# Two transformer blocks on one core: the start addresses of TensorE's large operands become multiples of 256 bytes

## The chip, the cores and the metric

The kernel runs on one core of one Trainium2 chip. The time is device microseconds of one execution of the whole program; it is given as the median of three runs. Below, TensorE is PE in the profile (PEld for its weight loads), VectorE is DVE, ScalarE is ACT, GpSimd is POOL and SyncE is SP.

## The reference, cut to what matters

512 tokens of width 1024 go through two blocks in fp32. The first block has a mixer (S5 and SSD), cross attention over 256 memory tokens, and a feed-forward layer of width 2816; the second has an HGRN2 and a forgetting-attention mixer and a mixture of 16 experts of width 512. What carries most of the work are plain products of activations and weights:

```
proj = rmsnorm(x, mix_norm_w) @ w_in          # 1024 x 2828
x = x + concat(y_s5, y_ssd) @ w_out           # 1024 x 1024
q = h @ wq; k = mem_n @ wk; v = mem_n @ wv    # 1024 x 1024 each
x = x + (silu(causal_dwconv(gv[:, :FF])) * gv[:, FF:]) @ w_down,  gv = h @ w_up
u = rms_norm(x) @ w_in_2
for e in range(16):
    h = silu(t @ w_gate[e]) * (t @ w_up[e])
    y = y + gates[:, e:e+1] * (h @ w_down[e])
```

## The kernel before

An fp32 product is made of three fp32r products. Each operand is split into a high part, its fp32r rounding, and a low part, the fp32 value less the high part: w_hi and w_lo for weights, h_hi and h_lo (or h2_hi and h2_lo, a_hi and a_lo, m_hi and m_lo, xh and xl, hh and hl) for activations. The product is high by high, low by high and high by low, accumulated in one bank of PSUM. In `pe_fm` (L430) these are L447, L448 and L449: 128 x 128 weights are stationary, and 512 columns of activations (256 for the memory) are the moving operand. In `pe_tm` (L454) at L466 to L468 it is the other way round, with 256 columns of weights moving. In the experts (`pe_part`, L3015) 128 x 128 of the gathered rows are stationary and 512 columns of weights move, at L3025 to L3027.

Weights come in slots of 2048 fp32 per partition (1 MB over 128 partitions). SyncE loads slot g into one of three buffers w_raw; ScalarE makes the high part of it into one of two buffers w_hi (`act_split`, L363), VectorE the low part into w_lo (`dve_split`, L371), and TensorE uses them. The waits form a ring: a load waits for the low part of three slots earlier, a high part for the load and for the last product of two slots earlier, a low part for the high part, a product for the low part. In the experts the six parts of an expert have a raw buffer each (three raw_b, three w_raw) and a split pair each: hi_b and lo_b for parts 0 and 1, w_hi and w_lo for parts 2 and 3, and the space of h_hi and h_lo for parts 4 and 5. GpSimd gathers the expert's rows (512 KB) for 12 of the 16 while the experts run, and stores 512 KB of results for each.

The order of instructions is written out engine by engine; no scheduler changes it. Addresses in SBUF are set by hand too: `Memory` (L171) places each tensor at the next multiple of 64 bytes, from offset 16512 up, and stages lay other tensors over the same space. The start of an operand within its tensor is a multiple of 512 bytes for all large products (and of 32 for the eight columns at L1838 to L1840), so the remainder of the tensor's offset modulo 256 is the remainder of the operand:

```
tensor                        offset before   modulo 256   used as
w_raw, w_hi, w_lo             16512 ...          128       weights
h_hi, h_lo, a_hi, m_hi, m_lo  90240 ...          128       activations (w_in, w_out, wo, w_out2; down; memory)
xh, xl                        73856 ...          128       gathered rows of the experts, stationary
h2_hi, h2_lo                  131392, 147776      64       activations (wq, up, all of w_in_2)
a_lo                          205120              64       down projection
raw_b, hi_b, lo_b             145856 ...         192       parts 0 and 1 of an expert
hh, hl                        221632, 223680     192       hidden values of an expert, stationary
```

Of the 1128 blocks of three products with 512 moving columns in `pe_fm`, 376 use h, 576 use h2 and 176 use a_hi and a_lo; the feed-forward has 352 of h2 and 176 of a. 64 blocks of the memory have 256 columns. `pe_tm` has 64 blocks with m as the stationary operand and 128 with h2.

## Time and profile before

| | before |
|---|---|
| median of 3 runs | 1576.21 us (1576.1 to 1580.75) |
| profiled execution | 1577.06 us, span 1575.9 us |
| instructions | 17703 |
| TensorE busy, matmul | 1464.7 us (93%) |
| TensorE busy, weight loads | 1162.5 us (74%) |
| VectorE, ScalarE, GpSimd busy | 1025.3, 759.0, 121.2 us |
| HBM read, written | 213.66 MB, 16.78 MB |

Busy time of a matmul runs from its start to its modelled end, and the next one starts before that end. How long a matmul holds TensorE is therefore read from the difference of two start times in the timeline, here called the pitch. The program's names are shown without the digits that number buffers, so that h_hi in a row can be h_hi or h2_hi; the stage tells which.

### The profile page before, as it was taken

Reading aid. Unit: us, or ns where it says so; the run is one execution under the profiler, and the core shown is the slowest. Engines: PE = TensorE matmul, PEld = TensorE weight load, DVE = VectorE, ACT = ScalarE, POOL = GpSimd, SP = SyncE. Lnnn points to the kernel's source line nnn. Section 1 sums busy time; section 2 is a strip of 40 time slices with the busy share of each in tenths; the row PEclk is TensorE's granted clock in tenths of the full one; section 3 lists DMA queues with packets and bytes.
Section 4 is the critical chain, followed back from the end, with each engine's and each line's share of the span. In section 5 each row is a group of like instructions: output and inputs, shape, how many; then the busy total and the mean of one; then the engine's idle time right before and its main releaser. Section 6 shows DMA issues by size and latency. Waiting matters only on the chain.

```text
span 1575.9 us, 17703 instructions
## 1 busy us (share of the span) xinstructions
PE 1464.7 (93%) x6975; PEld 1162.5 (74%) x6975; DVE 1025.3 (65%) x1361; ACT 759.0 (48%) x999; POOL 121.2 (8%) x148
## 2 busy tenths in 40 slices
PE   7899989889989999999999999899999799999981
PEld 5776668668767788888888778787758688888871
DVE  4888885555335555446555647865655898888976
ACT  5453354644334422222324543235564788887863
POOL 0500000000000000000000202300000101111012
PEclk9989999999999999999999999999999899999996
DMA  6212222202112332232223231111005799999975
GB/s 210 79 63 80 80 99 104 93 1 107 58 50 85 130 147 80 87 130 93 86 74 109 82 107 54 54 54 54 27 1 200 260 414 413 412 408 414 398 295 186
DMA packets 39330, 231.58 MB, mean 147 GB/s; under 512 B 4400, under 2 KB 5696, under 8 KB 17104
## 3 DMA queue, kind: packets, MB, share of 16 engines
q1 hardware_dynamic: 30640, 200.09, 33.9%
q0 software_dynamic: 7648, 27.87, 4.7%
q10 hardware_dynamic: 960, 2.49, 0.5%
q8 instruction: 56, 0.92, 0.2%
q14 instruction: 26, 0.21, 0.0%
HBM read 213.66 MB, written 16.78 MB: 146 GB/s over the span
## 4 chain that ended last, share of the span: by engine, by line
PE 74%; DVE 13%; ACT 6%; issue 4%; DMA 2%; POOL 0%; POOLq 0%; ACTq 0%; DVEq 0%
PE bank L447 14%; PE bank L448 14%; PE bank L449 14%; PE bank L3025 5%; PE bank L3027 5%; PE bank L3026 5%; PE bank L593 2%; DVE w_lo L374 2%; PE bank L466 1%; PE bank L467 1%; PE bank L468 1%; ACT w_hi L368 1%; PE bank L2275 1%; PE bank L2254 1%; PE bank L833 1%
## 5 line engine op out<-in xcount | busy, mean ns | idle before, releaser
L447 PE MATMUL bank<-h_hi,w_hi 128*128 128x512 f32 x952 | 387.1, 407 | 12.8 <-DVE w_lo L374 9.9
L448 PE MATMUL bank<-h_lo,w_hi 128*128 128x512 f32 x952 | 376.9, 396 | 0.0
L449 PE MATMUL bank<-h_hi,w_lo 128*128 128x512 f32 x952 | 376.8, 396 | 0.0
L374 DVE TENSOR_TENSOR w_lo<-w_raw,w_hi 128x2048 fp32r<-128x2048 f32 (+3 forms) x86 | 188.2, 2188 | 90.6 <-ACT w_hi L368 90.0
L447 PEld LDWEIGHTS bank<-h_hi,w_hi 128*128 128x128 f32 x952 | 180.6, 190 | 64.7 <-DVE w_lo L374 13.2
L449 PEld LDWEIGHTS bank<-h_hi,w_lo 128*128 128x128 f32 x952 | 180.4, 190 | 42.1
L448 PEld LDWEIGHTS bank<-h_lo,w_hi 128*128 128x128 f32 x952 | 180.9, 190 | 40.7 <-issue 2.2
L368 ACT ACTIVATE w_hi<-w_raw 128x2048 fp32r<-128x2048 f32 (+3 forms) x87 | 154.6, 1777 | 62.7 <-PE bank L449 62.7
L3210 DVE TENSOR_TENSOR h_lo<-w_raw,h_hi 128x2048 fp32r<-128x2048 f32 x32 | 73.1, 2291 | 13.8 <-ACT h_hi L3111 13.8
L3210 DVE TENSOR_TENSOR lo_b<-raw_b,hi_b 128x2048 fp32r<-128x2048 f32 x32 | 73.1, 2287 | 7.6 <-ACT hi_b L3111 7.6
L448 PE MATMUL bank<-a_lo,w_hi 128*128 128x512 f32 x176 | 69.0, 392 | 0.0
L1656 ACT ACTIVATE gc<-gc 128x512 f32<-128x512 f32 x22 | 13.9, 632 | 113.8 <-DVE gc L970 113.8
L447 PE MATMUL bank<-a_hi,w_hi 128*128 128x512 f32 x176 | 68.7, 390 | 0.0
L449 PE MATMUL bank<-a_hi,w_lo 128*128 128x512 f32 x176 | 68.5, 389 | 0.0
L3111 ACT ACTIVATE hi_b<-raw_b 128x2048 fp32r<-128x2048 f32 x32 | 61.2, 1912 | 5.3 <-PE bank L3027 3.5
L3111 ACT ACTIVATE h_hi<-w_raw 128x2048 fp32r<-128x2048 f32 x32 | 61.0, 1910 | 0.0
L3025 PE MATMUL bank<-h_hi,hh 128*128 128x512 f32 x128 | 52.6, 411 | 4.1 <-DVE hl L3240 2.6
L3025 PE MATMUL bank<-hi_b,xh 128*128 128x512 f32 x128 | 51.8, 405 | 1.4 <-DVE xl L3217 1.4
L3026 PE MATMUL bank<-h_hi,hl 128*128 128x512 f32 x128 | 51.3, 401 | 0.0
L3027 PE MATMUL bank<-h_lo,hh 128*128 128x512 f32 x128 | 51.2, 400 | 0.0
L1690 DVE TENSOR_TENSOR gc<-gc,bank 128x512 f32<-128x512 f32 x22 | 15.1, 688 | 55.1 <-PE bank L449 53.0
L3027 PE MATMUL bank<-lo_b,xh 128*128 128x512 f32 x128 | 50.2, 392 | 0.0
(592 smaller groups left out, 2843.9 us busy)
## 6 DMA issues: line engine op xcount, KB each, us to landing
w_raw<-in_params_dram SPq DMA_DIRECT2D x122, 1024.0 KB, 5.0
raw_b<-in_params_dram SPq DMA_DIRECT2D x51, 1024.0 KB, 7.7
w_raw<-in_params_dram SPq DMA_DIRECT2D x16, 704.0 KB, 4.1
result_rows<-osb POOLq DMA_DIRECT2D x16, 512.0 KB, 8.2
result_rows<-prm POOLq DMA_DIRECT2D x8, 512.0 KB, 3.2
xt<-in_x_t_dram POOLq DMA_DIRECT2D x1, 2048.0 KB, 9.3
scratch_rows<-htm SPq DMA_DIRECT2D x4, 512.0 KB, 3.0
out_dram<-pr SPq DMA_DIRECT2D x4, 512.0 KB, 2.6
```

The costliest lines, as they stand in the source:

```text
L368: A.activation(k.w_hi[:, g % SPLIT, 0:size], k.raw[:, g % RAW, 0:size], ACT.Copy).then_inc(s.w_hi, 1)
L374: V.tensor_tensor(k.w_lo[:, g % SPLIT, 0:size], k.raw[:, g % RAW, 0:size], k.w_hi[:, g % SPLIT, 0:size].bitcast(F32), ALU.subtract).then_i ...
L447: PE.matmul(ps, wh, hi[:, c, 0:width], start=c == 0, stop=False)
L448: PE.matmul(ps, wh, lo[:, c, 0:width], start=False, stop=False)
L449: m = PE.matmul(ps, wl, hi[:, c, 0:width], start=False, stop=c == parts - 1)
L466: PE.matmul(ps, xh, wh, start=c == 0, stop=False)
L593: return k.nc.tensor.transpose(out, in_, k.ident[0:n, 0:n])
L3025: PE.matmul(o, xh[:, k0 + c, :], wh, start=first and c == 0, stop=False)
L3026: PE.matmul(o, xl[:, k0 + c, :], wh, start=False, stop=False)
L3027: m = PE.matmul(o, xh[:, k0 + c, :], wl, start=False, stop=final and c == 3)
L3111: done(A.activation(w_hi[n], raws[n], ACT.Copy), "w", n, c)
L3210: done(V.tensor_tensor(w_lo[n], raws[n], w_hi[n].bitcast(F32), ALU.subtract), "w", n, c)
```

## The change

Class `Memory` gets a method `line` that moves the next offset up to a multiple of 256. It is called ahead of w_raw, ahead of xbc (whose space h2_hi and h2_lo share), and ahead of hi_b. The small tensors row, eps and rt go to the gap in front of w_raw. w_hi and w_lo, each one tensor with two buffers, become two tensors each at the same distance. gates, slot_of, table, act_scrap, ss and pri go behind the hidden values of the experts, and L, eoff and qi into the space of the masks tri and stri, whose last reader is TensorE at L1854. The engines' programs are the same, instruction by instruction and wait by wait; operands change their address, and w_hi and w_lo their names.

```
tensor                        offset after    modulo 256
w_raw, w_hi, w_lo             16896 ...            0
h_hi, h_lo, a_hi, m_hi, m_lo  90624 ...            0
xh, xl                        74240 ...            0
h2_hi, h2_lo                  131584, 147968       0
a_lo                          205312               0
raw_b                         145600             192
hi_b, lo_b                    170240 ...           0
hh, hl                        221440, 223488       0
```

```diff
--- before.py
+++ after.py
@@ -32,6 +32,7 @@
 OVER = MAXCH - E
 SLOT_TILES = MAXCH + 1
 SMALL = -1.0e30
+LINE = 256
 
 
 
@@ -186,6 +187,9 @@
         assert self.at <= self.end, (name, self.at, self.end)
         return t
 
+    def line(self):
+        self.at = (self.at + LINE - 1) // LINE * LINE
+
 
 class Core:
     def __init__(self, nc, ins, out, dram):
@@ -198,21 +202,25 @@
         self.bank = [nc.alloc_psum_tensor(f"bank{i}", [P, 512], F32) for i in range(8)]
         self.act_slot = self.dve_slot = 0
         m = Memory(nc, 16512)
+        self.row, self.eps, self.rt = m("row", [P, NROWS]), m("eps", [P, 1]), m("rt", [P, 4, TT])
+        m.line()
         self.raw = m("w_raw", [P, RAW, SLOT])
-        self.w_hi, self.w_lo = m("w_hi", [P, SPLIT, SLOT], F32R), m("w_lo", [P, SPLIT, SLOT], F32R)
+        self.w_hi, self.w_lo = [[m(f"{n}{i}", [P, SLOT], F32R) for i in range(SPLIT)] for n in ("w_hi", "w_lo")]
         x_at = m.at
         self.xt = m("xt", [P, DB, T])
         h_at = m.at
         self.hi, self.lo = m("h_hi", [P, DB, T], F32R), m("h_lo", [P, DB, T], F32R)
-        self.prm, self.row = m("prm", [P, NCOLS]), m("row", [P, NROWS])
+        self.prm = m("prm", [P, NCOLS])
         self.wr = m("w_router", [P, DB, 20])
-        self.ident, self.ones, self.tri, self.stri = (m(n, [P, P]) for n in ("ident", "ones", "tri", "stri"))
-        self.eps = m("eps", [P, 1])
+        self.ident, self.ones = (m(n, [P, P]) for n in ("ident", "ones"))
+        tri_at = m.at
+        self.tri, self.stri = (m(n, [P, P]) for n in ("tri", "stri"))
         base = m.at
 
 
 
         self.rs, self.dtr = m("rs", [P, T]), m("dtr", [P, TT, SSD_H])
+        m.line()
         xbc_at = m.at
         self.xbc, self.sz = m("xbc", [P, XBC_B, T]), m("sz", [P, 6, T])
         kv_at = m.at
@@ -304,19 +312,21 @@
         m = Memory(nc, x_at, h_at)
         self.xh, self.xl = m("xh", [P, 2, DB, P], F32R), m("xl", [P, 2, DB, P], F32R)
         m = Memory(nc, base)
-        self.xtm, self.gates, self.slot_of = m("xtm", [P, TT, D]), m("gates", [P, 2, TT]), m("slot_of", [P, 2, TT], I32)
-        self.table, self.act_scrap, self.rt = m("table", [P, OVER + 2], I32), m("act_scrap", [P, 2]), m("rt", [P, 4, TT])
+        self.xtm = m("xtm", [P, TT, D])
         inner = m.at
         self.raw_b = m("raw_b", [P, 3, SLOT])
+        m.line()
         self.hi_b, self.lo_b = m("hi_b", [P, 2, SLOT], F32R), m("lo_b", [P, 2, SLOT], F32R)
         rows = m.at
         self.xg, self.osb = m("xg", [P, 2, D]), m("osb", [P, 2, D])
         hidden = m.at
         self.hid = m("hid", [P, EH])
         self.hh, self.hl = m("hh", [P, EH // P, P], F32R), m("hl", [P, EH // P, P], F32R)
-        self.ss, self.pri, self.eoff = m("ss", [P, TT, DB]), m("pri", [P, 4]), m("eoff", [P, 2, E])
-        self.qi, self.qf = m("qi", [P, E], I32), m("qf", [P, E])
-        self.L, self.r4 = m("L", [P, TT, 20]), m("r4", [P, 6, TT, 4])
+        self.gates, self.slot_of, self.table = m("gates", [P, 2, TT]), m("slot_of", [P, 2, TT], I32), m("table", [P, OVER + 2], I32)
+        self.act_scrap, self.ss, self.pri = m("act_scrap", [P, 2]), m("ss", [P, TT, DB]), m("pri", [P, 4])
+        after_tri = Memory(nc, tri_at, tri_at + 4 * P)
+        self.L, self.eoff, self.qi = after_tri("L", [P, TT, 20]), after_tri("eoff", [P, 2, E]), after_tri("qi", [P, E], I32)
+        self.qf, self.r4 = m("qf", [P, E]), m("r4", [P, 6, TT, 4])
         self.r16 = m("r16", [P, 6, TT, E])
         self.tokid, self.tok_f, self.tok = m("tokid", [P, TT], I32), m("tok_f", [P, TT]), m("tok", [P, SLOT_TILES], I32)
         self.tok_next, self.rk, self.over = m("tok_next", [P, 1], I32), m("rk", [P, 4, 2, TT]), m("over", [P, OVER + 1])
@@ -348,7 +358,7 @@
         return self.row[:, slice(*ROWS[name])].rearrange("p (o h) -> p o h", o=1).broadcast_to([P, t, h])
 
     def w(self, g, at, n):
-        return self.w_hi[:, g % SPLIT, at:at + n], self.w_lo[:, g % SPLIT, at:at + n]
+        return self.w_hi[g % SPLIT][:, at:at + n], self.w_lo[g % SPLIT][:, at:at + n]
 
 
 
@@ -365,13 +375,13 @@
     A.wait_ge(k.w_load[g % RAW], 16 * (g // RAW + 1))
     if g >= SPLIT:
         A.wait_ge(s.gemm, FINAL_BLOCK[g - SPLIT] + 1)
-    A.activation(k.w_hi[:, g % SPLIT, 0:size], k.raw[:, g % RAW, 0:size], ACT.Copy).then_inc(s.w_hi, 1)
+    A.activation(k.w_hi[g % SPLIT][:, 0:size], k.raw[:, g % RAW, 0:size], ACT.Copy).then_inc(s.w_hi, 1)
 
 
 def dve_split(k, g):
     V, s, size = k.nc.vector, k.s, SIZES[g]
     V.wait_ge(s.w_hi, g + 1)
-    V.tensor_tensor(k.w_lo[:, g % SPLIT, 0:size], k.raw[:, g % RAW, 0:size], k.w_hi[:, g % SPLIT, 0:size].bitcast(F32), ALU.subtract).then_inc(s.w_lo, 1)
+    V.tensor_tensor(k.w_lo[g % SPLIT][:, 0:size], k.raw[:, g % RAW, 0:size], k.w_hi[g % SPLIT][:, 0:size].bitcast(F32), ALU.subtract).then_inc(s.w_lo, 1)
 
 
 def act_split_half(k, g, half):
@@ -381,7 +391,7 @@
     if half == 0:
         A.wait_ge(k.w_load[g % RAW], 16 * (g // RAW + 1))
         A.wait_ge(s.gemm, FINAL_BLOCK[g - SPLIT] + 1)
-    m = A.activation(k.w_hi[:, g % SPLIT, half * n:half * n + n], k.raw[:, g % RAW, half * n:half * n + n], ACT.Copy)
+    m = A.activation(k.w_hi[g % SPLIT][:, half * n:half * n + n], k.raw[:, g % RAW, half * n:half * n + n], ACT.Copy)
     if half:
         m.then_inc(s.w_hi, 1)
         k.act_slot += 1
@@ -395,7 +405,7 @@
     if half == 0:
         V.wait_ge(s.w_hi, g + 1)
     at = slice(half * n, half * n + n)
-    m = V.tensor_tensor(k.w_lo[:, g % SPLIT, at], k.raw[:, g % RAW, at], k.w_hi[:, g % SPLIT, at].bitcast(F32), ALU.subtract)
+    m = V.tensor_tensor(k.w_lo[g % SPLIT][:, at], k.raw[:, g % RAW, at], k.w_hi[g % SPLIT][:, at].bitcast(F32), ALU.subtract)
     if half:
         m.then_inc(s.w_lo, 1)
         k.dve_slot += 1
@@ -2908,7 +2918,7 @@
 
 def moe_parts(k):
     raws = [k.raw_b[:, i, :] for i in range(3)] + [k.raw[:, i, :] for i in range(3)]
-    w_hi, w_lo = ([x[:, i, :] for i in range(2)] + [w[:, i, :] for i in range(2)] + [flat2(h[:, 4 * i:4 * i + 4, :]) for i in range(2)]
+    w_hi, w_lo = ([x[:, i, :] for i in range(2)] + [w[i][:, :] for i in range(2)] + [flat2(h[:, 4 * i:4 * i + 4, :]) for i in range(2)]
                   for w, h, x in ((k.w_hi, k.hi, k.hi_b), (k.w_lo, k.lo, k.lo_b)))
     return raws, w_hi, w_lo
```

## Rows read from the trace of the kernel before

**Rows 1.** the page's first part: busy us (share of the span) xinstructions of TensorE
```profile
PE 1464.7 (93%) x6975; PEld 1162.5 (74%) x6975; DVE 1025.3 (65%) x1361; ACT 759.0 (48%) x999; POOL 121.2 (8%) x148
```

**Rows 2.** the chain that ended last, shares of the span by line
```profile
by line: PE bank L447 14.3%; PE bank L448 14.0%; PE bank L449 13.9%; PE bank L3025 5.0%; PE bank L3027 4.9%; PE bank L3026 4.9%; issue 4.1%; PE bank L593 2.5%; DVE w_lo L374 2.3%; PE bank L466 1.4%; PE bank L467 1.2%; PE bank L468 1.2%; ACT
```

**Rows 3.** two windows (us): busy time of each engine, granted clock, DMA share, GB/s
```profile
600.00:900.00 300.00, 300.00 (x1293) 242.60 (x1292) 161.80 (x180) 91.32 (x95) 5.42 (x11) 1.00 0.27 90
...
1300.00:1440.00 140.00, 140.00 (x657) 115.36 (x656) 124.56 (x79) 112.65 (x95) 18.34 (x16) 1.00 1.01 411
```

**Rows 4.** the page's groups: operands, shapes, count | busy, mean ns | idle before
```profile
L3210 DVE TENSOR_TENSOR h_lo<-w_raw,h_hi 128x2048 fp32r<-128x2048 f32 x32 | 73.1, 2291 | 13.8 <-ACT h_hi L3111 13.8
L3210 DVE TENSOR_TENSOR lo_b<-raw_b,hi_b 128x2048 fp32r<-128x2048 f32 x32 | 73.1, 2287 | 7.6 <-ACT hi_b L3111 7.6
...
L449 PE MATMUL bank<-a_hi,w_lo 128*128 128x512 f32 x176 | 68.5, 389 | 0.0
...
L3025 PE MATMUL bank<-h_hi,hh 128*128 128x512 f32 x128 | 52.6, 411 | 4.1 <-DVE hl L3240 2.6
```

**Rows 5.** timeline of TensorE (start, duration, us), output projection of the first mixer
```profile
352.19 0.39 PE L448 MATMUL bank<-h_lo,w_hi 128*128 128x512 f32 x1
...
368.51 0.39 PE L448 MATMUL bank<-h_lo,w_hi 128*128 128x512 f32 x1
```

**Rows 6.** timeline of TensorE, up projection
```profile
606.88 0.39 PE L448 MATMUL bank<-h_lo,w_hi 128*128 128x512 f32 x1
...
623.21 0.39 PE L449 MATMUL bank<-h_hi,w_lo 128*128 128x512 f32 x1
```

**Rows 7.** timeline of TensorE, down projection
```profile
664.17 0.39 PE L447 MATMUL bank<-a_hi,w_hi 128*128 128x512 f32 x1
...
677.90 0.39 PE L447 MATMUL bank<-a_hi,w_hi 128*128 128x512 f32 x1
```

**Rows 8.** timeline of TensorE, one expert's parts
```profile
1300.37 0.40 PE L3026 MATMUL bank<-h_hi,hl 128*128 128x512 f32 x1
...
1305.74 0.39 PE L3025 MATMUL bank<-w_hi,xh 128*128 128x512 f32 x1
...
1311.19 0.40 PE L3025 MATMUL bank<-hi_b,xh 128*128 128x512 f32 x1
...
1313.96 0.38 PE L593 MATMUL bank<-ident,hid 128*128 128x128 f32 x2
```

**Rows 9.** timeline of TensorE, products of 256 columns
```profile
253.10 0.28 PE L466 MATMUL bank<-w_hi,m_hi 128*128 128x256 f32 x1
...
254.54 0.28 PE L466 MATMUL bank<-w_hi,m_hi 128*128 128x256 f32 x1
...
938.27 0.28 PE L468 MATMUL bank<-w_lo,h_hi 128*128 128x256 f32 x1
...
940.99 0.28 PE L468 MATMUL bank<-w_lo,h_hi 128*128 128x256 f32 x1
```

**Rows 10.** timeline of TensorE, products with 8 stationary columns
```profile
926.00 0.40 PE L1838 MATMUL bank<-h_hi,w_hi 128*8 128x512 f32 x1
...
931.33 0.39 PE L1840 MATMUL bank<-h_hi,w_lo 128*8 128x512 f32 x1
```

**Rows 11.** timeline of TensorE, plain fp32 products, two merged in a row
```profile
396.19 0.59 PE L1431 MATMUL bank<-kt,qt 128*128 128x256 f32 x2
396.62 0.59 PE L1432 MATMUL bank<-kt,qt 128*128 128x256 f32 x2
```

**Rows 12.** transfers: 40 slices of 1204 to 1216 us, and issues of 1300 to 1440
```profile
GB/s 0 0 0 0 191 246 27 164 382 382 437 410 382 437 437 437 437 410 355 410 437 382 410 410 437 437 437 410 437 437 437 437 437 410 437 437 437 437 437 219
...
raw_b<-in_params_dram SPq DMA_DIRECT2D x24, 1024.0 KB, 8.4
w_raw<-in_params_dram SPq DMA_DIRECT2D x23, 1024.0 KB, 8.0
```

**Rows 13.** waits of ScalarE for loads, 1250 to 1505 us: total, times, longest
```profile
ACT hi_b L3111 <- DMA raw_b<-in_params_dram: 1.7, 1, 1.7
```

## The prediction, made before the changed kernel had run

> **What bounds the kernel now.** I read the page first, then the chain that ended last, the windows, the timeline of TensorE at its finest, and last the weight transfers of the expert stage. TensorE is busy for 93% of the span [rows 1], but matmuls are pipelined, so that share does not say what is late. The chain does: the three lines of the fp32r products with columns of activations (L447 to L449) hold 14.3 + 14.0 + 13.9 = 42.2% of it, the three of the experts (L3025 to L3027) 14.8%, the three of the values (L466 to L468) 3.8% [rows 2]. That is 665, 233 and 60 us of 1575.9. In the feed-forward stage, 600 to 900 us, TensorE is busy for 300.00 of 300 us at granted clock 1.00, while VectorE and ScalarE have 162 and 91 us of work; between 1300 and 1440 us it is 140.00 of 140 us, but there the DMA share is 1.01 as well [rows 3]. So the pitch of the matmuls, from one start to the next, decides nearly all of the time; the mean durations of 389 to 411 ns [rows 4] overlap and are not the pitch.
>
> The pitch is not one number. The page drops digits from names, so "h_hi" is h_hi in some stages and h2_hi in others, and the code has to say which. With remainders of the start address modulo 256, moving operand first:
> - (128, 128), h against w, 72 steps: 368.51 - 352.19 = 16.32 us, 226.7 ns [rows 5].
> - (64, 128), h2 against w, 70 steps: 16.33 us, 233.3 ns [rows 6].
> - down projection, two of three with a_hi at 128 and one with a_lo at 64, 60 steps: 13.73 us, 228.8 ns [rows 7]; (2 x 226.7 + 233.3) / 3 = 228.9, so the parts explain the mixture.
> - experts [rows 8]: (128, 192), the first 23 steps, 233.5 ns; (128, 128), the next 24, 227.1; (192, 128), the last 12, 230.8.
> - 256 columns: (128, 128) 12 steps 120.0 ns, (128, 64) 24 steps 113.3 ns [rows 9].
>
> **What a 256-byte start is worth.** No product here starts at remainder 0 on both sides, so its pitch must be bounded. Plain fp32 does 256 columns in 0.43 / 2 = 215 ns [rows 11], that is twice the columns' worth at the same clock, so a stream of 512 column steps can pass in 215 ns when the operand is wanted at half the rate; its operands stand at remainder 64 and it does not suffer. That is the floor. At 2.4 GHz, the level that a granted clock of 1.00 means, 226.7 and 233.3 ns are 544 and 560 cycles, 32 and 48 over 512; 120.0 ns for 256 columns is 288, again 32 over; 113.3 is 272, 16 over. So the surplus comes in steps of 16 cycles, 64 bytes of a full-rate operand, does not grow with the width, and changes when either remainder changes. Even 8 stationary columns leave it: 23 steps of h2 against a w whose remainder runs through eight values take 231.7 ns each [rows 10], so it belongs to the moving operand's start at least in part. No rule of one operand alone gives all five levels; what the pairs share is that each has at least one operand off the boundary. My reading is that an operand that starts inside a 256-byte line pays for the line's part that it does not use; at remainder 0 nothing is left to pay and the pitch is the floor, 216 ns with rounding. Other ends: 226.7, the best full-width row here, if the surplus depends on the difference between the two operands and 32 cycles are its value at equal remainders; and 240.0, one more step of 6.7 ns beyond the worst row, if 0 is the worst remainder. The nearest row that speaks below 226.7 is the 113.3 (16 cycles over, less than 32), which shows that 32 is no fixed price of a change of weights. I take 216.
>
> The Trainium skill says otherwise in one place: "SBUF — State Buffer", Specifications, gives 16-byte cachelines as what full bandwidth depends on; all four remainders are multiples of 16, so by that rule the change would do nothing (1576 us), and the pitches of 226.7 and 233.3 ns speak against it as the only rule. Its "TensorE: Matmul & The Clock Gate", Back-to-back issue gap, gives N / 2.4 + 2.5, 215.8 ns for 512 columns: the fp32r rows are 11 to 18 ns off it, and by it all of that could go.
>
> **The change part by part.** Instructions, waits, queues and counts are the same; only addresses and names move.
> 1. *Feed-forward, 600 to 900 us.* TensorE is always busy, the pitch is a mean of about (2 x 233.3 + 228.8) / 3 = 231.8 ns (352 blocks of h2 to 176 of a). 300 x (231.8 - 216) / 231.8 = 20.4 us, all on the path; VectorE's 162 us has room. If TensorE's cover were gone, VectorE is next, far off.
> 2. *The other products at L447 to L449.* Their mean pitch over the program, by 376 blocks of h, 576 of h2 and 176 of a, is 230.4 ns. Of the chain's 665 us, 23 are 192 narrow ones of the memory (0.120 us each) and 300 the feed-forward, so 342 us x 14.4 / 230.4 = 21.4.
> 3. *256 columns.* The chain's 60 us of L466 to L468 and the 23 above, at some 119 ns now and half the floor, 109.5, then: 83 x 9.5 / 119 = 6.6.
>  Outside the feed-forward the chain goes over from TensorE to the splits on ScalarE and VectorE and back (a split waits for the last product of the block two slots earlier, L367, and the product for the split). Where TensorE gets faster, another path ends a little sooner after it; I take 80% of 21.4 + 6.6: 22.4.
> 4. *Experts.* Mean pitch (227.1 + 230.8 + 233.5) / 3 = 230.5; 233 us x 14.5 / 230.5 = 14.7 if nothing else binds. But an expert is 84 matmuls, 140 / 657 x 84 = 17.9 us [rows 3], and moves 6 MB of weights (6.29 million bytes) and, while rows are still gathered, twice 512 KB: 7.34 million in 17.9 us, 410 GB/s, and the row of the window says 411 [rows 3]. A pitch of 216 wants 17.9 - 72 x 0.0145 = 16.9 us, 435 GB/s. The weight queue alone reached 437 in slices of the first expert loads [rows 12], so the ceiling lies between 411 and 437. At 411 the gain is the prefetch in hand alone: loads are no reason for ScalarE's waits but once, 1.7 us [rows 13], and land some us before use, so about 5; at 437 it is 14.7. I take 10, since the last experts gather nothing.
> 5. *Splits and loads.* h_lo from w_raw (both at 128) takes 2291 ns, lo_b from raw_b (both at 192) 2287 [rows 4]: the elementwise engines do not feel the remainder, 0. Loads land after 8.0 us into w_raw (128) and 8.4 into raw_b (192) [rows 12], which differ by their neighbours in the queue; w_raw at 0 I cost at 0, bounded by the gap of 411 to 437 above.
> 6. *Small tensors.* L, eoff and qi take the place of the triangular masks, gates and the table move up, row, eps and rt down. They are written after the masks' last use in both orders; same waits, 0.
>
> Sum: 20.4 + 22.4 + 10 = 52.8. The profiled execution is 1577.06 us (span 1575.9), the median of the runs 1576.21, 0.85 less: 1577.06 - 52.8 - 0.85 = 1523.4, say 1523.
>
> **Rivals.**
> - *Equal remainders, not zero ones.* The surplus is 32 cycles whenever both operands start alike, so every product goes to 226.7 ns. For: (128, 128) is a level of its own, and 64 against 128 and 128 against 192, both a difference of 64, cost the same 48 cycles. Against: (128, 64) lies under it and 8-column weights at all remainders keep the price. Gain 642 x 3.7 / 230.4 = 10.3 and 233 x 3.8 / 230.5 = 3.8, less 1 where 256 columns rise to 120: 13, time 1563.
> - *The place, not the remainder.* h2, a_lo, hi_b and hh lie above 131 KB in the partition, h, w, xh and a_hi below 123 KB, so that distance or bank could be what is slow; everything moves by under 400 bytes and stays there. Against: h2 as stationary gives the lowest pitch of the 256-column rows. Time 1576, the change does not do what it says.
> - *Collision.* Both operands start in the same 64 bytes of a 256-byte line, and weights are fetched while columns stream; if 0 is the worst meeting point, the next step is 240.0 ns. 642 x 9.6 / 230.4 + 233 x 9.5 / 230.5 = 36 us more: 1612. It decides from a pitch of 230.5 ns up. For: equal remainders cost 120 against 113.3 at 256 columns. Against: at 512 columns the equal ones are the best.
>
> **How the numbers follow.** Zero surplus 0.60 (1523; its own range 1510 to 1540, from experts capped at their 5 or not at all, from 70 to 100% kept in the mixed stages, and from a pitch up to 220); equal remainders, or a surplus only partly gone, 0.25 (1545 to 1564); place 0.08 (1576); collision 0.07 (1612). A measurement of this kernel tells 0.3%, 4.7 us, from no change. Faster 0.85, same 0.08, slower 0.07. The range takes in the first two cases less their tails: 1509 to 1565.
>
> **What would show it.** Right: in the feed-forward the start-to-start pitch is within 2 ns of 216 for h2 and for a alike, the stretch is some 20 us shorter, 256-column steps take 109 to 110 ns, and in the experts TensorE begins to wait, last for ScalarE or a load, at 411 to 437 GB/s. Wrong: a pitch of 226 to 227 everywhere (equal remainders), 233 unchanged (place), or above 233 (collision); and if the pitch is 216 but the time over 1540, the splits took over outside the feed-forward.

## The result, and the profile after

The changed kernel takes 1565.41 us (median of 5 runs, 1564.06 to 1569.59), the one before 1576.27 us beside it (5 runs, 1576.1 to 1580.75): a ratio of 0.9933 with the interval 0.9917 to 0.9949. It is faster by 0.7%, 11 us; forecast were 53. The rival "equal remainders" had put it at 1563.

The profiled execution, the fastest of the five, took 1564.06 us (span 1562.8), 13.0 less than before's 1577.06. The page of the changed kernel, its first part and the groups that answer to [rows 1, 4] (the code lies 10 lines lower, L447 is L457 and L3025 is L3035):

```profile
PE 1454.9 (93%) x6975; PEld 1163.5 (74%) x6975; DVE 1024.0 (66%) x1361; ACT 760.2 (49%) x999; POOL 122.1 (8%) x148
...
L3220 DVE TENSOR_TENSOR h_lo<-w_raw,h_hi 128x2048 fp32r<-128x2048 f32 x32 | 73.2, 2291 | 12.3 <-ACT h_hi L3121 10.4
L3220 DVE TENSOR_TENSOR lo_b<-raw_b,hi_b 128x2048 fp32r<-128x2048 f32 x32 | 73.1, 2285 | 5.9 <-ACT hi_b L3121 5.9
L459 PE MATMUL bank<-a_hi,w_lo 128*128 128x512 f32 x176 | 68.5, 389 | 0.0
L3035 PE MATMUL bank<-h_hi,hh 128*128 128x512 f32 x128 | 51.8, 404 | 4.1 <-DVE hl L3250 2.6
```

The page says little. TensorE has 9.8 us less busy time and the same 93%, and the means of the matmuls, 389 to 404 ns, are hardly lower: each matmul runs on into the next one, so its duration is not its pitch. The splits h_lo and lo_b take 2291 and 2285 ns, as before. The chain by line, which answers to [rows 2]:

```profile
by line: PE bank L457 14.3%; PE bank L458 13.9%; PE bank L459 13.9%; PE bank L3035 4.9%; PE bank L3037 4.9%; PE bank L3036 4.9%; issue 4.1%; PE bank L603 3.0%; DVE w_lo L384 2.3%; PE bank L476 1.4%; ACT w_hi L378 1.3%; PE bank L477 1.3%; PE
```

The chain has the same owners with the same shares. The products of columns of activations still hold 42.1%, so no other engine has taken over. The two windows of [rows 3]:

```profile
600.00:900.00 300.00, 299.95 (x1322) 247.10 (x1321) 164.85 (x185) 93.46 (x98) 12.71 (x26) 1.00 0.28 94
1300.00:1440.00 140.00, 140.00 (x665) 116.29 (x665) 125.88 (x80) 114.22 (x96) 18.56 (x16) 1.00 1.01 417
```

In the feed-forward 1322 matmuls fit into 300 us instead of 1293, still with TensorE busy throughout, so a mean of 226.9 ns instead of 232.0. A pitch of 216 would have shown 1389. In the experts 665 instead of 657 fit into 140 us. All transfers together are at 417 GB/s instead of 411, and no engine waits for a load in the experts: the 1.7 us of [rows 13] are gone.

The timeline of TensorE in the up projection (75 steps lie between the first two rows) and in the down projection (60 steps between the last two), which answer to [rows 6, 7]; the columns are start and duration in us:

```profile
604.65 0.39 PE L458 MATMUL bank<-h_lo,w_hi 128*128 128x512 f32 x1
...
621.65 0.39 PE L458 MATMUL bank<-h_lo,w_hi 128*128 128x512 f32 x1
...
664.04 0.39 PE L459 MATMUL bank<-a_hi,w_lo 128*128 128x512 f32 x1
...
677.64 0.39 PE L459 MATMUL bank<-a_hi,w_lo 128*128 128x512 f32 x1
```

17.00 / 75 = 226.7 ns and 13.60 / 60 = 226.7 ns. What took 233.3 and 228.8 now takes what h against w took before [rows 5], and not less. One expert, which answers to [rows 8] (24, 24 and 12 steps):

```profile
1289.95 0.47 PE L3035 MATMUL bank<-h_hi,hh 128*128 128x512 f32 x1
...
1295.52 0.39 PE L3035 MATMUL bank<-w_hi,xh 128*128 128x512 f32 x1
...
1300.96 0.39 PE L3035 MATMUL bank<-hi_b,xh 128*128 128x512 f32 x1
...
1303.69 0.60 PE L603 MATMUL bank<-ident,hid 128*128 128x128 f32 x4
```

The three stretches are 5.57, 5.44 and 2.73 us: 232.1, 226.7 and 227.5 ns. The first, right behind the transposes, is not yet at 226.7. And h2 as stationary operand against 256 columns, 24 steps, which was 113.3 ns [rows 9]:

```profile
927.91 0.28 PE L478 MATMUL bank<-w_lo,h_hi 128*128 128x256 f32 x1
...
930.79 0.28 PE L478 MATMUL bank<-w_lo,h_hi 128*128 128x256 f32 x1
```

It is 2.88 / 24 = 120.0 ns now: this product became slower, as the rival "equal remainders" had said.

**Where the time went.** The same matmul was looked up in both traces at each border; the table gives how much longer (+) or shorter a stretch became against before, in us. The columns to the right are the experiments below, each of one profiled execution.

| stretch of before, us | changed | all64 | all128 | h2_moved | experts_only | h2_plus |
|---|---|---|---|---|---|---|
| 0 to 300 | -2.9 | -0.7 | -0.4 | -1.6 | -2.8 | 0.0 |
| 300 to 600 | -1.9 | -2.8 | -1.7 | -2.8 | +2.1 | -2.2 |
| 600 to 900, feed-forward | -6.1 | -6.1 | -6.1 | -6.1 | 0.0 | +0.5 |
| 900 to 1235 | +1.2 | +1.8 | +1.2 | +1.9 | +0.2 | -0.5 |
| 1235 to 1521, experts | -2.8 | -4.0 | -4.0 | -0.1 | -4.1 | -2.3 |
| 1521 to the end | -0.7 | -1.0 | -0.2 | -0.9 | +1.9 | -0.5 |

The feed-forward's -6.1 is the same in all four kernels in which h2 and w start alike. Most of the other differences between columns are the granted clock, not the addresses. Three windows of the kernel before (the third number from the end is the granted clock):

```profile
250.00:300.00 50.00, 47.12 (x310) 39.26 (x308) 24.54 (x28) 24.17 (x50) 0.00 (x0) 0.97 0.24 84
930.00:940.00 10.00, 9.98 (x78) 8.58 (x77) 5.14 (x6) 5.50 (x6) 0.00 (x0) 1.00 0.30 107
940.00:950.00 10.00, 10.00 (x91) 10.00 (x90) 9.16 (x29) 6.19 (x9) 0.00 (x0) 1.00 0.30 107
```

The same three of the changed kernel:

```profile
250.00:300.00 50.00, 46.43 (x314) 37.90 (x312) 26.25 (x30) 24.90 (x53) 0.00 (x0) 1.00 0.25 85
930.00:940.00 10.00, 10.00 (x80) 10.00 (x80) 9.58 (x25) 4.74 (x7) 0.00 (x0) 0.91 0.21 88
940.00:950.00 10.00, 8.81 (x69) 8.56 (x68) 4.96 (x5) 4.51 (x5) 3.40 (x1) 0.92 0.29 105
```

From 250 to 300 us the changed kernel was granted 1.00 against 0.97, which is the 1.6 us that it won there, and all64, all128 and h2_plus, at 0.97 like before, won nothing there. From 930 to 950 it was granted 0.91 and 0.92 against 1.00, so that for some us of these 20 it ran at 1.2 and not at 2.4 GHz. That is where the +1.2 of the fourth row comes from. Around the fall TensorE did products of 256 columns with its weight loads busy throughout (10.00 of 10 us), and in the kernel before the same work ran at 1.00. The last 1.2 us between the changed kernel's experts and those of all64 are 0.92 against 1.00 from 1500 to 1521 us. So a difference of a stage under 2 us says something of the addresses only where the clock is the same.

### The profile page after: what moved, and what is told of

Read it like the earlier page. It is cut to its first block, busy times and chain, and to the rows that moved or that the text cites. A ratio compares the mean times of both kernels' runs of the same rounds, so it can differ in the third digit from the quotient of the medians.

```text
span 1562.8 us, 17703 instructions
## 1 busy us (share of the span) xinstructions
PE 1454.9 (93%) x6975; PEld 1163.5 (74%) x6975; DVE 1024.0 (66%) x1361; ACT 760.2 (49%) x999; POOL 122.1 (8%) x148
## 4 chain that ended last, share of the span: by engine, by line
PE 74%; DVE 13%; ACT 6%; issue 4%; DMA 2%; POOL 0%; POOLq 0%; ACTq 0%; DVEq 0%
PE bank L457 14%; PE bank L458 14%; PE bank L459 14%; PE bank L3035 5%; PE bank L3037 5%; PE bank L3036 5%; PE bank L603 3%; DVE w_lo L384 2%; PE bank L476 1%; ACT w_hi L378 1%; PE bank L477 1%; PE bank L478 1%; PE bank L2264 1%; PE bank L2285 1%; PE bank L843 1%
## 5 line engine op out<-in xcount | busy, mean ns | idle before, releaser
L457 PE MATMUL bank<-h_hi,w_hi 128*128 128x512 f32 x952 | 384.4, 404 | 11.4 <-DVE w_lo L384 8.5
L457 PEld LDWEIGHTS bank<-h_hi,w_hi 128*128 128x128 f32 x952 | 181.0, 190 | 60.6 <-DVE w_lo L384 11.7
L3220 DVE TENSOR_TENSOR h_lo<-w_raw,h_hi 128x2048 fp32r<-128x2048 f32 x32 | 73.2, 2291 | 12.3 <-ACT h_hi L3121 10.4
L3220 DVE TENSOR_TENSOR lo_b<-raw_b,hi_b 128x2048 fp32r<-128x2048 f32 x32 | 73.1, 2285 | 5.9 <-ACT hi_b L3121 5.9
L457 PE MATMUL bank<-a_hi,w_hi 128*128 128x512 f32 x176 | 68.5, 389 | 0.0
L3035 PE MATMUL bank<-h_hi,hh 128*128 128x512 f32 x128 | 51.8, 404 | 4.1 <-DVE hl L3250 2.6
L3035 PE MATMUL bank<-hi_b,xh 128*128 128x512 f32 x128 | 51.6, 403 | 1.5 <-DVE xl L3227 1.5
L3035 PE MATMUL bank<-w_hi,xh 128*128 128x512 f32 x128 | 49.9, 390 | 0.0
```

The source lines that it names most:

```text
L457: PE.matmul(ps, wh, hi[:, c, 0:width], start=c == 0, stop=False)
L3035: PE.matmul(o, xh[:, k0 + c, :], wh, start=first and c == 0, stop=False)
L3220: done(V.tensor_tensor(w_lo[n], raws[n], w_hi[n].bitcast(F32), ALU.subtract), "w", n, c)
```

## The experiments

**All pairs of remainders (grid).** A kernel of its own: triples of products as in the kernel, 96 of each pair of moving and stationary start. a, b, c, d are remainders 0, 64, 128, 192; the sets lie where h and w lie in the kernel.

```python
for m in REMAINDERS:
    for s in REMAINDERS:
        n += 1
        triples(k, n % 8, m, s, 512, 32)
```

> This kernel leaves the whole model out: it loads x, writes it out again, and has TensorE do the kernel's triples of fp32r products (high by high, low by high, high by low) for all 16 pairs of start remainders modulo 256, first with 512 and then with 256 moving columns, 96 products a pair, nothing else running. Operands named a, b, c, d begin at remainder 0, 64, 128, 192; m is moving, s stationary. Theory 1, the difference decides (moving less stationary, modulo 256): the four equal pairs all have a pitch of 226.7 ns at 512 columns and 120.0 at 256; the pairs (64,128), (128,192), (0,64), (192,0) share 233.3; the pairs (128,64), (64,0), (192,128), (0,192) share one lower level at 256 columns, 113 to 118. Theory 2, the absolute remainder modulo 128 decides: (0,0), (128,128), (0,128), (128,0) are at 226.7, all pairs with 64 or 192 at about 233. Theory 3, the place in the partition and not the remainder: all 16 pairs within 2 ns, since their places differ by some KB only.

Four of the sixteen groups, from its timeline of TensorE (names: m moving, s stationary, h or l, then the letter of the remainder). The rows stand in pairs of 68, 69, 71 and 69 steps:

```profile
70.06 0.39 PE L34 MATMUL bank<-mla,shb 128*128 128x512 f32 x1
...
85.93 0.39 PE L33 MATMUL bank<-mha,shb 128*128 128x512 f32 x1
...
90.81 0.39 PE L33 MATMUL bank<-mha,shc 128*128 128x512 f32 x1
...
106.85 0.39 PE L33 MATMUL bank<-mha,shc 128*128 128x512 f32 x1
...
133.70 0.39 PE L33 MATMUL bank<-mhb,sha 128*128 128x512 f32 x1
...
149.95 0.39 PE L35 MATMUL bank<-mhb,sla 128*128 128x512 f32 x1
...
155.00 0.39 PE L33 MATMUL bank<-mhb,shb 128*128 128x512 f32 x1
...
170.64 0.39 PE L33 MATMUL bank<-mhb,shb 128*128 128x512 f32 x1
```

Moving 0 against stationary 64 takes 15.87 / 68 = 233.4 ns, 0 against 128 232.5, 64 against 0 228.9, 64 against 64 226.7. The whole square, each value from its own group:

| moving less stationary start | pairs | 512 columns, ns (cycles at 2.4 GHz) |
|---|---|---|
| 0 | (0,0) (64,64) (128,128) (192,192) | 226.7 (544) |
| +64 | (64,0) (128,64) (192,128) (0,192) | 228.9 (549) |
| 128 | (0,128) (64,192) (128,0) (192,64) | 232.4 (558) |
| -64 | (0,64) (64,128) (128,192) (192,0) | 233.4 (560) |

Here the difference, modulo 256, decides at 512 columns: the four pairs of each line share nothing else and agree within 0.1 ns. No pair is near 216, and (0,0) is not special. The operands lay where h and w lie, and the pitch followed their remainders, which speaks against distance or bank as the cause (the rival "place"); h2_moved below settles it for h2 itself. 240 (the rival "collision") is no group's pitch. At 256 columns the equal pairs take 120.0 ns, the unequal ones 117.8 or 118.7 and two of them, (64,128) and (128,192), 113.3: here equality is the worst, as [rows 9] had shown, and the difference alone does not decide, since (0,64) and (192,0) have the same one and take 117.8.

**Finer steps, columns and widths (grid2).** One pair of operands, the stationary start moved by 16 bytes from 0 to 1008, then fewer stationary columns, then narrower products, then two operand pairs in turn (product by product, in six combinations), 24 of each.

```python
for s in range(0, 1024, 16):
    fine(k, s, 0)
for cols in (8, 32, 64, 96):
    for s in (0, 64, 128, 192):
        columns(k, s, cols)
for width in (128, 256, 384, 448):
    for s in (0, 64, 128, 192):
        widths(k, s, width)
for pair in ((0, 64, 0, 0), (0, 64, 0, 64), (0, 64, 64, 0), (0, 128, 0, 0), (0, 128, 0, 128), (0, 128, 128, 0)):
    last = two(k, *pair)
```

> This kernel leaves the whole model out: it loads x, writes it out again, and has TensorE repeat one fp32r product with one moving and one stationary operand, nothing else running. First the stationary operand's start goes from 0 to 1008 bytes in steps of 16 (24 products each, moving operand at 0, 512 columns); then three moving starts of 256, 512 and 1024; then 8, 32, 64 and 96 stationary columns at 0, 64, 128, 192; then 128, 256, 384 and 448 moving columns; then two operand pairs in turn. Theory 1, the difference modulo 256 decides: the fine sweep repeats every 256 bytes, with 544 cycles (226.7 ns) at 0, 256, 512 and 768 and 549 to 560 at 64, 128 and 192. Theory 4, the surplus is the weight load's reads colliding with the moving stream: it falls with the stationary columns, to 518 cycles or less (216 ns) at 8 columns. Theory 5, it belongs to the start of each moving stream: 8 columns keep 544 and the surplus is the same 32 cycles from 128 to 512 moving columns.

Its timeline merges equal products in a window into a row, so that the pitch is the duration less one product's 0.39, over the count less 1. The rows are stationary starts 0, 16 and 32, then 8 stationary columns at 0 and at 64, then 384 columns at 0:

```profile
24.22 5.15 PE L27 MATMUL bank<-mv,st 128*128 128x512 f32 x22
...
29.66 5.38 PE L27 MATMUL bank<-mv,st 128*128 128x512 f32 x23
...
34.64 5.76 PE L27 MATMUL bank<-mv,st 128*128 128x512 f32 x24
...
395.94 5.60 PE L27 MATMUL bank<-mv,st 128*8 128x512 f32 x24
...
401.61 5.47 PE L27 MATMUL bank<-mv,st 128*8 128x512 f32 x23
...
506.94 3.80 PE L27 MATMUL bank<-mv,st 128*128 128x384 f32 x21
```

4.76 / 21 = 226.7, 4.99 / 22 = 226.8, 5.37 / 23 = 233.5: a difference of 16 bytes is still free, to either side (start 240 settles at 226.7 too), and 32 costs the full price. The pattern repeats every 256 bytes, and the moving start at 256, 512 and 1024 gives 226.7 again. Between the four remainders of the square lie other values, up to 234.2 at start 96, and starts 128 apart run at 233.3 here and not at the 232.4 of the square.

With 8 stationary columns it is 5.21 / 23 = 226.5 at equal starts and 5.08 / 22 = 230.9 at 64 apart, so the 231.7 of [rows 10] is a mixture of mostly unequal starts and says nothing of a price that stays. At equal starts, 128, 256, 384, 448 and 512 moving columns take 111.7, 120.0, 173.3, 202.3 and 226.7 ns; that is 32 cycles over the columns at 256, 384 and 512, 38 at 448 and 140 at 128, where the pitch is hardly shorter than with 256. So theory 4 fails at 8 stationary columns, which leave the pitch at 226.7 and not at 216, and theory 5 holds from 256 to 512 columns but for the 448.

Equality is not the best everywhere. The next rows are 96 stationary columns at 0 and at 64, then 448 moving columns at 0 and at 192, then two rows of pairs in turn, the first with both operands at 0 and then both at 64, the second with both at 0 and then both at 128:

```profile
462.34 5.45 PE L27 MATMUL bank<-mv,st 128*96 128x512 f32 x23
...
467.86 5.41 PE L27 MATMUL bank<-mv,st 128*96 128x512 f32 x23
...
523.39 4.63 PE L27 MATMUL bank<-mv,st 128*128 128x448 f32 x22
...
538.00 4.36 PE L27 MATMUL bank<-mv,st 128*128 128x448 f32 x21
...
548.32 5.49 PE L47 MATMUL bank<-mv,st 128*128 128x512 f32 x23
...
565.06 5.20 PE L47 MATMUL bank<-mv,st 128*128 128x512 f32 x22
```

With 96 stationary columns equal starts take 5.06 / 22 = 230.0 ns and starts 64 apart 5.02 / 22 = 228.2; 64 columns are like that (230.0 at equal starts, 228.3 with the stationary start at 192), and 32 have 231.7. With 448 moving columns one product lasts 0.36 us, so equal starts take 4.27 / 21 = 203.3 (202.3 in the second half) and a stationary start at 192 takes 4.00 / 20 = 200.0. And products that each have equal starts, but at 0 and at 64 in turn, take 5.10 / 22 = 231.8; at 0 and at 128 in turn they take 4.81 / 21 = 229.0 (228.3 in the second half). So 226.7 needs more than equal starts within a product: with 128 stationary and 512 moving columns it was measured where all products in a row have the same remainder, as they have in the changed kernel.

**The same change to remainder 64 or 128 (all64, all128).** The starts are as equal as in the changed kernel, but none of them is a multiple of 256 bytes.

```diff
-LINE = 256
+LINE, REMAINDER = 256, 64
-        self.at = (self.at + LINE - 1) // LINE * LINE
+        self.at = (self.at - REMAINDER + LINE - 1) // LINE * LINE + REMAINDER
```

> The changed kernel with every operand that it puts at a multiple of 256 put at 64 past one instead, so that all differences stay 0. Theory 1, the difference decides: the time of the changed kernel, 1565 us, pitch 226.7 ns in the feed-forward. Theory 2, a start at a multiple of 128 or 256 is what counts: pitch 233.3 everywhere, which is 230.4 to 233.3 for the 642 us of the chain and 230.5 to 233.3 for its 233 us of the experts, 11 us more than before, 1587 us.

> The same with all at 128 past a multiple of 256. Theory 1: 1565 us. Theory 2: 1565 us as well. If the boundary of 256 bytes itself is worth something beside the difference, this one is slower than the changed kernel, by up to 5 us.

Measured: all64 1564.4 us (1563.09 to 1564.99), ratio to before 0.9917 with 0.9903 to 0.993; all128 1563.7 us (1562.78 to 1565.87), 0.9912 with 0.9897 to 0.9928. The feed-forward of all64:

```profile
600.00:900.00 300.00, 299.94 (x1321) 247.16 (x1320) 164.91 (x185) 93.75 (x98) 12.71 (x26) 1.00 0.27 93
```

1321 matmuls in 300 us, as in the changed kernel. all128 is not slower than the changed kernel either. So a multiple of 256 bytes is worth nothing by itself; what the change brings comes from starts that are equal.

**One part at a time (h2_moved, experts_only).** The first is the kernel before with one line more, which moves h2 and a_lo from 64 to 128, where the weights are, and leaves the experts alone:

```diff
+        m.at += 64
         xbc_at = m.at
```

The second is all128 with h2 and a_lo put back to 64, so that only the experts' operands are equal:

```diff
         m.line()
+        m.at += 192
         xbc_at = m.at
```

> The kernel before with one edit: 64 bytes are skipped ahead of xbc, which puts h2_hi, h2_lo and a_lo at 128 like w, and leaves the experts' operands (hi_b, lo_b, hh, hl at 192) as they were. Theory 1: 576 blocks x 3 x 6.7 ns and 176 x 3 x 2.1 ns, 12.7 us of pitch, of which some 80 to 85% on the chain: 1566 us; the experts' part of the change is then worth 1 us or less, since transfers bind there. If the experts carry a share in proportion to their pitch, this one lies at 1567 to 1569. Theory 3, the place: 1576.

> The changed kernel with all operands 128 past a multiple of 256, except that 192 bytes are skipped ahead of xbc: h2_hi, h2_lo and a_lo are at 64 again, 64 bytes below the weights' remainder, as before the change, and the experts' operands agree. Difference theory: the feed-forward keeps its old pitches of 233.3 and 228.8 ns, the experts take 17.73 us each in place of 17.90; 3 to 4 us faster than before, 1573 to 1574. If the gain of the change came from somewhere else than the difference between h2 and w (new places of the small tensors, w_hi and w_lo as two tensors each), this one keeps most of it: 1565 to 1568.

Measured: h2_moved 1568.23 us (1563.98 to 1569.02), ratio 0.9939 with 0.9925 to 0.9952; experts_only 1573.35 us (1571.85 to 1575.64), 0.9976 with 0.9964 to 0.9987. The two windows of h2_moved:

```profile
600.00:900.00 300.00, 299.95 (x1321) 247.10 (x1320) 165.28 (x185) 93.37 (x99) 12.71 (x26) 1.00 0.27 93
1300.00:1440.00 140.00, 140.00 (x660) 115.37 (x659) 125.15 (x79) 113.00 (x94) 17.78 (x15) 1.00 1.01 413
```

And of experts_only:

```profile
600.00:900.00 300.00, 300.00 (x1293) 242.56 (x1292) 162.43 (x181) 91.33 (x95) 5.96 (x12) 1.00 0.26 90
1300.00:1440.00 140.00, 140.00 (x662) 116.20 (x661) 125.85 (x80) 114.21 (x95) 18.18 (x16) 1.00 1.01 415
```

The first has the changed kernel's feed-forward (1321) and before's experts nearly (660 in the window; matched by instruction, they are equal to 0.1 us), the second before's feed-forward (1293) and faster experts (662). 9 us for h2 and a_lo and 4 for the experts add up to the 13.5 of all128, so nothing is left for the small tensors, which move in experts_only as well. h2_moved was expected at 1566 if the transfers bind in the experts, and at 1567 to 1569 if the experts gain in proportion to their pitch; it is at 1568. It also answers "place": 64 bytes further, in the same part of the partition, h2 runs at the changed kernel's pitch.

**The sign of the difference (h2_plus).** all128 with h2 and a_lo at 192, 64 above the weights instead of 64 below as before. By the square the pitch of h2 should be 228.9 and not 233.4.

```diff
         m.line()
+        m.at += 64
         xbc_at = m.at
```

> The same with 64 bytes skipped ahead of xbc: h2_hi, h2_lo and a_lo are at 192, 64 bytes above the weights' remainder of 128. If the sign counts as in the grid: products of 512 columns with h2 at 228.9 ns, 2.2 more than at equal remainders, 1728 x 2.2 + 176 x 2.2 = 4.2 us, 3.6 of them on the chain; those of 256 columns with h2 stationary at 113.3 to 117.8 in place of 119.7, 0.4 to 1.2 us back on the chain; 2 to 3 us over the version with all at 128, 1566 to 1567. If the size of the difference alone counts: 233.3 ns and the time of the one with h2 at 64, 1573 to 1574.

Measured 1570.53 us (1567.35 to 1572.03), ratio 0.9949 with 0.9935 to 0.9963: between what was expected for a sign that counts and for one that doesn't. The timeline has the reason, first in the up projection at 605 us (74 steps), then in the next one at 704 us (69 steps), the same tensors and the same remainders:

```profile
605.03 0.39 PE L458 MATMUL bank<-h_hi,w_hi 128*128 128x512 f32 x1
...
621.97 0.39 PE L460 MATMUL bank<-h_hi,w_lo 128*128 128x512 f32 x1
...
703.78 0.40 PE L459 MATMUL bank<-h_lo,w_hi 128*128 128x512 f32 x1
...
719.88 0.40 PE L459 MATMUL bank<-h_lo,w_hi 128*128 128x512 f32 x1
```

16.94 / 74 = 228.9 ns, and 16.10 / 69 = 233.3 ns. So a difference of +64 has two pitches that last. Up to 631 us all steps are at 228.9. The down projection from 634 us on, in which a_hi is equal to the weights and a_lo is 64 above, takes a mean of 232 (228.8 before, with a_lo 64 below), and the up projection that follows it without a gap stays at 233.3 for 110 us. The next products of h2, from 878 us on, come behind a step of 0.33 us, and they are at 229 again. The square's 228.9 holds only for what came before it there. At equal starts, with 512 moving columns, the pitch returned to 226.7 in each stage looked at, whatever preceded it. The down projection also shows that the pitch of a mixture is not the mean of its parts: (2 x 226.7 + 228.9) / 3 would be 227.4, not 232.

It is so at 256 columns too: experts_only has h2 and w 64 apart as before, and by single starts it runs at 117.8 ns the products that took 113.3 before.

**After transposes (grid3).** Why are the experts' products not at 226.7 at once? 8 fp32 transposes, then 24 products, six times, for the stationary start at 0 and the moving one at 0, 64, 128 and 192. No other engine works.

```python
for r in range(6):
    for i in range(8):
        k.nc.tensor.transpose(k.bank[7][:, 0:P], k.id[:, :], k.id[:, :])
    same(k, bank, s, P, m, 512, n)
```

> This kernel leaves the whole model out, as the other two grids. For the moving operand at 0, 64, 128 and 192 bytes past the stationary one's remainder it does 24 products of 512 columns, then six times 8 transposes of 128 x 128 in fp32 and 24 products, then six times 8 transposes and 48 products. If the settled pitch needs a run-up after every change of kind, the products behind the transposes begin at 230 to 236 ns at difference 0 and reach 226.7 after 6 to 15, with a cost of 30 to 80 ns per run-up; the groups of 48 then end at 226.7 all. If the experts' 229 ns in the changed kernel has another cause (transfers or the splits on the other engines reading SBUF), the products behind the transposes are at 226.7 from the second on, since nothing else runs here.

Two rounds at equal starts, from its timeline (L36 are the transposes, L29 the products):

```profile
28.71 1.04 PE L36 MATMUL bank<-id 128*128 128x128 f32 x8
29.51 5.70 PE L29 MATMUL bank<-mv,st 128*128 128x512 f32 x24
35.05 1.03 PE L36 MATMUL bank<-id 128*128 128x128 f32 x8
35.84 5.71 PE L29 MATMUL bank<-mv,st 128*128 128x512 f32 x24
```

(5.70 - 0.39) / 23 = 230.9 ns, where 226.7 would be the settled pitch: the products need about 0.10 us more after transposes, 0.09 to 0.13 in the twelve rounds at equal starts, where 0.03 to 0.08 were expected. By single starts, the first step takes 313 to 318 ns, and then the pitch is 226.7 at once in one round, after 3 steps in six and after 10, at 224 to 236, in five. No other engine works here, so the run-up needs none. The first stretch of the expert above has the steps of the rounds of ten but for one of 229: 314, 233, 236, 224, 231, 236, 228, 233, 230 ns, then 226.7. So the 0.13 us by which it (5.57 us) is over 24 x 226.7 = 5.44 is this run-up.

## Why the prediction was wrong

**The step that failed** is "What a 256-byte start is worth", and in it "at remainder 0 nothing is left to pay and the pitch is the floor, 216 ns". The surplus of 16 to 48 cycles was read rightly from the rows, and that it does not grow with the width is borne out at 256, 384 and 512 columns (grid2; 448 have 38 cycles). The mean of parts that it found in the down projection [rows 7] fits by its figure, but h2_plus shows that such a mean need not hold. And the rule made of the surplus, that each operand pays for the part of the line that it does not use, was on no row: the rows showed five pairs, none with a remainder 0. grid and all64 show what is in its place: for 128 stationary and 512 moving columns the difference of the two starts decides, its value 0 had already been measured, and its price, 226.7 ns, was already in the kernel in h against w [rows 5].

Two rows had been used against the right theory, and both misled. The 8-column products [rows 10] have a stationary start that runs through eight values, so their 231.7 ns is a mean over mostly unequal pairs; with 8 columns and equal starts it is 226.5. And the 113.3 ns at 256 columns [rows 9] showed that 32 cycles can be undercut at that width; it said nothing of 512, where no pair in the square is under 544 cycles. The plain fp32 products [rows 11] gave a floor for a stream of another rate, which no fp32r product of any start came near. They were also misread: L1431 issues 16 products, one for each of 16 steps, and the trace of the kernel before has 32 records of it:

```profile
L1431 PE MATMUL bank<-kt,qt 128*128 128x256 f32 x32 | 9.9, 390 | 1.2 <-ACT pa L1464 1.2
```

So a product of 256 columns is the two records of a row of [rows 11] and holds TensorE for 0.43 us; 215 ns is half a product, and not what 256 columns cost. The Trainium skill's "TensorE: Matmul & The Clock Gate", Back-to-back issue gap, gives N / 2.4 + 2.5, which is 215.8 ns for 512 columns, as the gap of one matmul by itself; here the best is 10.9 ns over that, with a weight load in each product.

**The terms, one by one:**
- *Feed-forward*: 20.4 forecast, 6.1 measured; the rival's pitch gives 300 x (231.8 - 226.7) / 231.8 = 6.6. That all of it is on the path was right: TensorE is busy 299.95 of 300 us.
- *The other products at L447 to L449*: 21.4 forecast (17 with the 80%), some 3 measured (all64 and h2_moved, from 375 to 600 us, where they and the kernel before were granted 1.00 alike); h against w was already at 226.7 and could gain nothing. From 900 to 930 us, again at 1.00 in both, 0.7 more went. The rest is under the clock's spread.
- *256 columns*: a gain of 6.6 forecast; they became slower where h2 is the stationary operand, 113.3 to 120.0.
- *Experts*: 10 forecast, from 14.7 with a limit of the transfers. Measured are 2.8 from 1235 to 1521 us, where the clock was before's, and 4 between the medians of experts_only and before; the rival had 3.8. The limit of the transfers was never reached: 417 GB/s, and no engine waits for a load. Of the three parts of an expert, before's 5.68, 5.45 and 2.77 us [rows 8, and the first step before them] became 5.57, 5.44 and 2.73: of the 0.16 us (24 x 6.7 ns) that the stretch with a difference of -64 could win, 0.11 came, since its run-up after the transposes is nine steps long now and was one step before. What is missing from the 10 is the pitch of 216, which no stretch reached.
- *Splits, loads, small tensors*: forecast 0 and measured 0 (2291 and 2285 ns; loads into w_raw land after 8.0 us as before).
- *Rivals*: "place" and "collision" are refuted, the first by grid (the same places, other remainders, other pitches) and h2_moved (the same place, 64 bytes on, the best pitch), the second by grid (no group over 233.4). "Equal remainders" had 0.25, together with a surplus only partly gone, and was what happened: its three figures of 10.3, 3.8 and -1 against 9 (h2_moved), 4 (experts_only) and a slower stretch at 900 to 960 us of which the clock took the most. The way it was put, equal starts within each product, is too weak by grid2's pairs in turn, but in this kernel it makes no difference.

The sign of the change was right, and the reason given for the size was not. The range ended at 1565, just short of the median, and that end came from the rival: the leading case had a range of its own, 1510 to 1540.

**Not shown:** why the difference of the starts matters at all, and why 32 cycles stay at equal ones; why fewer stationary columns, 448 moving ones or remainders that change from product to product follow another order; why +64 has two lasting pitches and what enters it into either; why the run-up is 3 products long in one round and 10 in the next; and why the clock falls behind 930 us in all kernels with h2 moved (0.97 from 900 to 960 us) and neither in the kernel before nor in experts_only (1.00). The 120.0 ns are not it alone: h2_plus runs these products at 117.8 ns and falls too, to 0.88 from 940 to 950 us.

## What to carry to other kernels

Give the moving and the stationary operands of large fp32r products (128 stationary and 512 moving columns) all the same start modulo 256 bytes, rather than each an aligned one: 64 against 64 did as well as 0 against 0, and a tensor one slot (64 bytes) off costs up to 6.7 ns of 233 in each product. For other shapes measure first: at 256 and 448 moving columns, and at 64 and 96 stationary ones, an unequal pair was the best. When levels are read from rows and extended to a case that no row has, ask first for the rule that needs no new level: here the best pitch that some pair in the kernel already had was also the best that any pair showed. And a price seen where an operand's start varies is a mean over its starts, not a proof that the price is fixed.

## What was not expected of the hardware

- The pitch of fp32r products with 128 stationary and 512 moving columns goes by the difference of the starts modulo 256: 226.7 ns at 0 (and at 16 bytes to either side), 228.9 at +64, 232.4 or 233.3 at 128, 233.4 at -64. Equal starts that change from product to product (0 and 64 in turn) take 231.8.
- Products of 128 moving columns take 111.7 ns and of 256 columns 120.0, with a weight load each: half the width saves almost nothing.
- The same pair of starts can run for 100 us at 228.9 or at 233.3, depending on what ran before (h2_plus); the equal pair came back to one value in each stage looked at.
- The first start to start behind a run of fp32 transposes is 313 to 318 ns, and up to ten products pass before the pitch has settled (grid3, equal starts).
- Under 2 us, stages of two executions differ by the granted clock (0.97 against 1.00 over 50 us is the 1.6 us above), more than by the smaller effects of this change.
